# In the sliding-window attention stage, the gate's weight tile is taken ahead of the next head pair's scores on every engine

## The chip, the cores and the metric

The program runs on one core of one Trainium2 chip. The metric is the device time of one execution in microseconds (us). The engines named below are PE (TensorE, matrix products), DVE (VectorE), ACT (ScalarE), POOL (GpSimd) and SP (which issues the weight DMAs). Each engine works through its own list of instructions in order, and they meet only at semaphores. A difference under about 0.5% of the time (10.9 us) is not told apart from no change in this kernel.

## The reference

The program computes two blocks one after the other on 512 tokens of width 1024: first a block with a state-space branch, a recurrent branch and a memory attention, then a block of four layers (`second_block`). The change is in the second of those layers, a sliding-window attention with a gate. Cut to what matters:

```python
def sliding_window_attention(q, k, v, sinks, rel_bias):
    ...                                   # blocks of 128 queries see 256 keys
    s = jnp.einsum('bnqhgd,bnkhd->bnhgqk', qb, kb).astype(jnp.float32) * (HEAD_DIM ** -0.5)
    ...
    s = jnp.where(valid[None, :, None, None], s + bias, NEG_INF)
    sink = jnp.broadcast_to(sinks.astype(jnp.float32).reshape(SWA_KV_HEADS, grp, 1, 1), s.shape[:-1] + (1,))
    p = jax.nn.softmax(jnp.concatenate([s, sink], axis=-1), axis=-1)[..., :-1]
    o = jnp.einsum('bnhgqk,bnkhd->bnqhgd', p.astype(v.dtype), vb)
    return o.reshape(bsz, L, SWA_WIDTH)

def swa_branch(h, w_in, sinks, w_out, rel_bias):
    ...
    q, k, v, z = jnp.split(h @ w_in, [SWA_WIDTH, SWA_WIDTH + kv_w, SWA_WIDTH + 2 * kv_w], axis=-1)
    ...
    o = sliding_window_attention(q, k, v, sinks, rel_bias)
    return (o * jax.nn.silu(z)) @ w_out
```

There are 16 query heads of width 64, and 2 heads of keys and values. The gate is `silu(z)`, with `z` another 1024 columns of the same projection.

## The kernel before

All float32 weights come as "slabs" of 16 blocks of 128x128. SP loads a slab into a ring of three (L435). ACT copies it into a rounded high part (`ring_high`, L440) and DVE or POOL forms the remainder (`ring_low`, L445). A product of a weight tile with the activations is three matmuls for each of eight blocks (L483 to L485). A weight tile uses eight blocks, so a slab holds two tiles, and the split of a slab is issued behind every second tile (`split_high` on ACT, `split_low` on POOL in this stage). `split_high` waits until the tile that used the old high part has been computed.

`stage_swa` handles the heads as eight pairs j = 0 to 7 and is written out engine by engine, in a fixed order. Its parts for a pair are:

- scores(j), PE, L3061: query times key, into four PSUM banks `sb[j]`.
- logits(j), DVE, L3111 to L3122: scale and bias from PSUM into the tile `swa_s`, then maxima over keys (L3117, L3118) and three small operations. The last one, L3122, raises `mx`.
- exps(j), ACT, L3188 and L3193: exponentials with their sums. It waits for `mx` and raises `ex`.
- probs(j), DVE, L3127, L3128, L3131: divides by the sum. It waits for `ex` and raises `pn`.
- transposes(j), PE, L3079, wait for `pn`. ACT copies them to `swa_pt` (L3210, four copies), and PE multiplies them with the values (L3093) into the bank `ob[j]`. I call this last product PV(j).
- the gate's weight tile z(j), PE, L483 to L485, into bank `zb[j]`. DVE takes it out (evac_z, L1492), ACT makes the tanh (curve, L2899) and DVE the factor (L2904). The tanh has a single slot, so curve(j) waits for factor(j - 1).
- gated(j), DVE, L3144: output times factor, from `ob[j]`. Then ACT and DVE split the result (L2908, L2912) for the output projection, `gated_output`.

The scores of a pair are made two pairs ahead. In step j of the loop, PE does transposes(j), scores(j + 2), z(j + 2), PV(j). DVE does probs(j + 1), gated(j - 1), logits(j + 2), evac_z(j + 2), factor(j + 1), and the low part of j - 2. ACT does the four copies of pair j, exps(j + 2), the split of a slab when z(j + 2) ended one, curve(j + 2), and the high part of j - 1.

PSUM has eight banks, handed out in turn (`take_bank`), and a bank is reused only after its reader is done. In the steady steps the fourth score bank of pair j + 2 is the one that `ob[j - 1]` had, so the last quarter of the scores waits for gated(j - 1).

Of the kernel before, what the change touches and what calls it, by code (L numbers as in the profile page):

```python
# [28 lines left out]
KD = DM // P  # L29
# [3002 lines left out]
def stage_swa(C, L):  # L3032
# [3 lines left out]
    sb, pb, ob, zb = [[C.take_bank() for _ in range(TC)] for _ in range(2)], [], [], [C.take_tile(KD) for _ in range(2)]  # L3036
    for j in range(NJ):
        pb.append([C.take_bank() for _ in range(TC)])
        if j + 2 < NJ:
            sb.append([C.take_bank() for _ in range(TC)])  # L3040
            zb.append(C.take_tile(KD))
        ob.append(C.take_bank())
    mx, ex, pn = C.reserve("mx", NJ), C.reserve("ex", NJ), C.reserve("pn", NJ)
    zr = C.reserve("swaz", 1)
# [1 line left out]
    with C.stage() as block:  # L3046
        @block.sync
        def _(sp):
            C.load_slabs(sp, block.slabs)

        @block.tensor
        def _(pe):
            def scores(j):

                for b, u in enumerate(sb[j]):
                    e = b // 2
                    C.open(pe, u)
                    for n in (2 * (b % 2), 2 * (b % 2) + 1):
                        lo = 0 if n else P
                        r = slice(64 * e, 64 * e + 64)  # L3060
                        mm = pe.matmul(C.bank[u.b][:, n % 2 * 256 + lo:n % 2 * 256 + 256], L.Q[r, j, n * P:(n + 1) * P],  # L3061
                                       L.K[r, 0, (n - 1) * P + lo:(n + 1) * P], start=True, stop=True)
                    mm.then_inc(C.bank_full[u.b], 1)

            seen = set()
            C.read(pe, L.v_uses[-1])
            C.read(pe, L.k_tile)
            scores(0)
            scores(1)
            for j in range(2):  # L3070
                C.gemm(pe, zb[j], C.H.tiles(KD), seen)
            for j in range(NJ):
                pe.wait_ge(pn.sem, pn.at(j))
                for n, u in enumerate(pb[j]):
                    C.open(pe, u)
                    for e in range(2):
                        for kt in range(0 if n else 1, 2):
                            a = (2 * e + kt) * P
                            mm = pe.transpose(C.bank[u.b][:, a:a + P], L.S[:, j % 2, n, e, kt * P:(kt + 1) * P], C.ident[:])  # L3079
                    mm.then_inc(C.bank_full[u.b], 1)  # L3080

                if j + 2 < NJ:
                    scores(j + 2)
                    C.gemm(pe, zb[j + 2], C.H.tiles(KD), seen)
                u = ob[j]
                C.open(pe, u)
                for n in range(TC):
                    C.read(pe, pb[j][n])
                    for e in range(2):
                        first = 0 if n else 1  # L3090
                        for kt in range(first, 2):
                            a = (2 * e + kt) * P
                            mm = pe.matmul(C.bank[u.b][64 * e:64 * e + 64, n * P:(n + 1) * P],  # L3093
                                           L.V[:, n - 1 + kt, 64 * e:64 * e + 64], L.PT[:, n, a:a + P],
                                           start=(kt == first), stop=(kt == 1))
                mm.then_inc(C.bank_full[u.b], 1)

        @block.vector
        def _(dve):
# [35 lines left out]
            def evac_z(j):  # L3135
                u = zb[j][0]
                C.full(dve, u)
                times_root(dve, j, C.bank[u.b]).then_inc(C.bank_read[u.b], 1)
# [21 lines left out]
            for j in range(NJ):  # L3160
                if j + 1 < NJ:
                    probs(j + 1)
                if j > 0:
                    gated(j - 1)
                if j + 2 < NJ:
                    logits(j + 2)
                    evac_z(j + 2)
                if j + 1 < NJ:
                    gate.factor_on_dve(dve, j + 1, L.Z[:, j + 1, :], 1.0)
                if j > 1:  # L3170
                    gate.low_on_dve(dve, j - 2)
# [12 lines left out]
        def _(act):  # L3184
# [11 lines left out]
            def curve(j):  # L3196
                C.read(act, zb[j][0])
                gate.curve_on_act(act, j, L.Z[:, j, :], ACT.Tanh, 0.5)
# [6 lines left out]
            for j in range(NJ):  # L3205
                for n, u in enumerate(pb[j]):
                    C.full(act, u)
                    lo = 0 if n else 1
                    v = lambda ap: ap.rearrange("p (e t k) -> p e t k", e=2, t=2)[:, :, lo:2, :]
                    act.activation(v(L.PT[:, n, :]), v(C.bank[u.b][:]), ACT.Copy).then_inc(C.bank_read[u.b], 1)  # L3210
                if j + 2 < NJ:
                    exps(j + 2)
                    C.split_high(act, zb[j + 2][0])
                    curve(j + 2)
                if j > 0:
                    gate.high_on_act(act, j - 1)
            gate.high_on_act(act, NJ - 1)
# [650 lines left out]
```

## Time and profile before

| what | us |
|---|---|
| median of 3 runs | 2182.3 (2181.11 to 2189.23) |
| profiled execution, its own time | 2188.14 |
| its span | 2186.0 |
| PE / DVE / ACT / POOL busy in the span | 1996.6 / 1341.6 / 850.3 / 466.5 |

The profiled execution takes 2.14 us more than its span. The mean granted TensorE clock was 0.963 of full speed. The stage of the change lies between 1421 and 1536 us of the span, about 5% of it. A row of the timeline gives start, length, engine, line, operation, output and inputs, a count where equal instructions were merged, and in brackets how long the engine had been idle before and what ended the idle time. In rows of PE a matmul of the scores or of PV counts twice.

### The profile page before, as it was taken

How to read it: one execution, taken by the hardware profiler on the slowest of the kernel's cores; microseconds unless marked ns; L12 is line 12 of the kernel's file. 1: busy time of each engine (PE TensorE's matmuls, PEld its weight loads, DVE VectorE, ACT ScalarE, POOL GpSimd, SP SyncE). 2: the span in 40 equal slices, each digit the busy share in tenths (PEclk: the TensorE clock that was granted, in tenths of full speed). 3: DMA queues.
4: the chain of work that ended last, by engine and by line, in shares of the span. 5: the costliest groups of instructions: out<-in, count | busy, mean ns of one | idle time of the engine just before them, and what ended most of it. 6: DMA issues, size and time to landing. Idle time of an engine off the chain costs nothing.

```text
span 2186.0 us, 24847 instructions
## 1 busy us (share of the span) xinstructions
PE 1996.6 (91%) x9910; PEld 1567.2 (72%) x9910; DVE 1341.6 (61%) x1926; ACT 850.3 (39%) x1228; POOL 466.5 (21%) x393
## 2 busy tenths in 40 slices
PE   4998888999999999999999899988989989899986
PEld 3777665788657888768797676866777756578865
DVE  5997885825639245445566454678386476738474
ACT  3324646412259224422232343355342344435332
POOL 5861110323248603024400101012001011100001
PEclk9999998999999999999999999999998999999998
DMA  3333331233322434434546626211221210123211
GB/s 129 125 145 121 129 112 61 80 118 122 124 96 97 154 111 159 173 87 135 183 132 148 156 78 123 78 58 40 71 107 58 97 39 20 39 77 125 97 58 58
DMA packets 63746, 225.20 MB, mean 103 GB/s; under 512 B 14144, under 2 KB 31216, under 8 KB 43280
## 3 DMA queue, kind: packets, MB, share of 16 engines
q1 hardware_dynamic: 22896, 162.54, 21.2%
q0 software_dynamic: 19760, 45.83, 7.1%
q10 hardware_dynamic: 20976, 15.26, 3.3%
q8 instruction: 78, 1.28, 0.2%
q14 instruction: 36, 0.29, 0.0%
HBM read 208.72 MB, written 14.81 MB: 102 GB/s over the span
## 4 chain that ended last, share of the span: by engine, by line
PE 64%; DVE 10%; ACT 5%; issue 3%; ACTq 1%; DMA 1%; POOL 0%; DVEq 0%; POOLq 0%
PE bank L483 18%; PE bank L484 18%; PE bank L485 18%; PE bank L482 2%; DVE ring_low L445 1%; PE bank L3295 1%; PE bank L3322 1%; ACT ring_high L440 1%; ACTq L2476 1%; ACT swa_s L3193 1%; PE bank L2000 1%; DVE lru_x L1914 1%; PE bank L619 1%; DVE swa_s L3111 1%; PE bank L3309 1%
## 5 line engine op out<-in xcount | busy, mean ns | idle before, releaser
L483 PE MATMUL bank<-h_high,ring_high 128*128 128x512 f32 x1248 | 508.3, 407 | 36.3 <-DVE ring_low L445 12.2
L445 DVE TENSOR_TENSOR ring_low<-ring,ring_high 128x2048 fp32r<-128x2048 f32 x136 | 329.5, 2423 | 325.3 <-ACT ring_high L440 325.1
L484 PE MATMUL bank<-h_low,ring_high 128*128 128x512 f32 x1248 | 495.2, 397 | 0.0
L485 PE MATMUL bank<-h_high,ring_low 128*128 128x512 f32 x1248 | 494.8, 396 | 0.0
L440 ACT ACTIVATE ring_high<-ring 128x2048 fp32r<-128x2048 f32 x145 | 277.3, 1913 | 514.4 <-PE bank L485 511.8
L483 PEld LDWEIGHTS bank<-h_high,ring_high 128*128 128x128 f32 x1248 | 240.8, 193 | 106.4 <-issue 40.3
L484 PEld LDWEIGHTS bank<-h_low,ring_high 128*128 128x128 f32 x1248 | 240.7, 193 | 53.1 <-issue 4.1
L485 PEld LDWEIGHTS bank<-h_high,ring_low 128*128 128x128 f32 x1248 | 239.8, 192 | 51.9
L445 POOL TENSOR_TENSOR ring_low<-ring,ring_high 128x2048 fp32r<-128x2048 f32 x9 | 44.3, 4925 | 385.2 <-ACT ring_high L440 385.2
L483 PE MATMUL bank<-gated_high,ring_high 128*128 128x512 f32 x256 | 104.3, 407 | 8.3 <-DVE sq L3584 5.0
L484 PE MATMUL bank<-gated_low,ring_high 128*128 128x512 f32 x256 | 102.0, 398 | 0.0
L485 PE MATMUL bank<-gated_high,ring_low 128*128 128x512 f32 x256 | 101.6, 397 | 0.0
L483 PEld LDWEIGHTS bank<-gated_high,ring_high 128*128 128x128 f32 x256 | 49.0, 192 | 22.3 <-issue 7.5
L483 PE MATMUL bank<-ring_high,h_high 128*128 128x512 f32 (+1 forms) x160 | 60.4, 378 | 3.5 <-ACT u_tok L2610 2.1
L3433 ACT ACTIVATE mla_s<-mla_s,mla_st 128x128 f32<-128x128 f32 (+1 forms) x64 | 36.0, 563 | 64.3 <-DVE mla_st L3345 62.1
L1213 ACT ACTIVATE sq<-bank 128x512 f32<-128x512 f32 x32 | 19.3, 602 | 104.4 <-PE bank L485 104.4
L484 PE MATMUL bank<-ring_low,h_high 128*128 128x512 f32 (+1 forms) x160 | 59.8, 374 | 0.0
L485 PE MATMUL bank<-ring_high,h_low 128*128 128x512 f32 (+1 forms) x160 | 59.7, 373 | 0.0
L484 PEld LDWEIGHTS bank<-gated_low,ring_high 128*128 128x128 f32 x256 | 49.0, 191 | 11.7 <-issue 1.0
L485 PEld LDWEIGHTS bank<-gated_high,ring_low 128*128 128x128 f32 x256 | 48.8, 191 | 11.4
L669 DVE SCALAR_TENSOR_TENSOR sq<-bank,cols,sq 128x511 f32<-128x511 f32 (+2 forms) x72 | 53.9, 749 | 2.5
L3295 PE MATMUL bank<-mla_k,mla_q 128*128 128x128 f32 (+3 forms) x128 | 40.9, 467 | 14.3 <-ACT mla_k L3424 14.3
(517 smaller groups left out, 3859.8 us busy)
## 6 DMA issues: line engine op xcount, KB each, us to landing
ring<-slabs SPq DMA_DIRECT2D x149, 1024.0 KB, 4.8
acs_rows<-acs_rows POOLq DMA_DIRECT2D x16, 512.0 KB, 4.9
s_outputs<-s_ca POOLq DMA_DIRECT2D x4, 1152.0 KB, 5.0
x<-xT SPq DMA_DIRECT2D x2, 2048.0 KB, 8.5
exp_acs<-acs_rows POOLq DMA_DIRECT2D x16, 256.0 KB, 8.8
s_b<-s_br POOLq DMA_DIRECT2D x8, 512.0 KB, 4.2
s_rows<-s_powers POOLq DMA_DIRECT2D x16, 256.0 KB, 6.7
s_inputs<-s_w POOLq DMA_DIRECT2D x8, 512.0 KB, 3.0
```

What stands on the lines that cost most here:

```text
L440: act.activation(self.ring_high[:, self.splits_before[s] % AHEAD, :], self.ring[:, s % RING, :], ACT.Copy)\
L445: dve.tensor_tensor(self.ring_low[:, s % RING, :], self.ring[:, s % RING, :], self.ring_high[:, self.splits_before[s] % AHEAD, :].bitcast( ...
L482: return pe.matmul(out, w, x, start=start, stop=stop)
L483: pe.matmul(out, w[0], x[0], start=start, stop=False)
L484: pe.matmul(out, w[0], x[1], start=False, stop=False)
L485: return pe.matmul(out, w[1], x[0], start=False, stop=stop)
L619: pe.matmul(C.bank[u.b][:, 0:n], C.ones[:], C.sq[:, i % 4, 0:n], start=(k == 0), stop=(k == len(grp) - 1)).then_inc(summed.sem, 1)
L669: ins = dve.scalar_tensor_tensor(out=acc[:, d:T], in0=x[:, 0:T - d], scalar=w(3 - d), in1=acc[:, d:T], op0=ALU.mult, op1=ALU.add)
L1914: dve.tensor_tensor_scan(L.XL[:, m, :], L.R[:, m, :], q, 0.0, ALU.mult, ALU.add)\
L2000: mm = pe.matmul(C.bank[u.b][:], L.V[:, mt, a:a + P], L.PT[:, mt, :], start=(mt == 0), stop=(mt == 1))
L3295: mm = pe.matmul(C.bank[u.b][:, 0:(i + 1) * P], L.Q[:, h, i * P:(i + 1) * P], L.K[:, h % 4, 0:(i + 1) * P], start=True, stop=True)
L3433: ins = act.activation(s, s, ACT.Exp, bias=st[:, 0, i:i + 1], accum_out=st[:, 1, i:i + 1])
```

## The change

Four places swap two neighbours each. The instructions are the same, 7246 rows on PE, 1522 on DVE and 779 on ACT before and after. POOL's and SP's lists do not change. Banks are handed out in the new order too.

```diff
         pb.append([C.take_bank() for _ in range(TC)])
         if j + 2 < NJ:
+            zb.append(C.take_tile(KD))
             sb.append([C.take_bank() for _ in range(TC)])
-            zb.append(C.take_tile(KD))
         ob.append(C.take_bank())
...
                 if j + 2 < NJ:
+                    C.gemm(pe, zb[j + 2], C.H.tiles(KD), seen)
                     scores(j + 2)
-                    C.gemm(pe, zb[j + 2], C.H.tiles(KD), seen)
                 u = ob[j]
...
                 if j + 2 < NJ:
+                    evac_z(j + 2)
                     logits(j + 2)
-                    evac_z(j + 2)
                 if j + 1 < NJ:
                     gate.factor_on_dve(dve, j + 1, L.Z[:, j + 1, :], 1.0)
...
                 if j + 2 < NJ:
-                    exps(j + 2)
                     C.split_high(act, zb[j + 2][0])
                     curve(j + 2)
+                    exps(j + 2)
                 if j > 0:
                     gate.high_on_act(act, j - 1)
```

On ACT, this is the order in a step whose z tile ends a slab (j = 1, 3 or 5), rows that go with -, rows that come with +. L440 is the split, L2899 the curve, L3188 and L3193 the exponentials, L3210 the copies.

```order
 L3210 ACTIVATE swa_pt_162<-bank 128x512 x3
+L440 ACTIVATE ring_high_54<-ring_52 128x2048
+L2899 ACTIVATE root_57<-swa_z_163 128x512
 L3188 ACTIVATE swa_st_164<-swa_st_164 128x8
 L3193 ACTIVATE swa_s_161,swa_st_164<-swa_s_161,swa_st_164 128x128 x2
 L3193 ACTIVATE swa_s_161,swa_st_164<-swa_s_161,swa_st_164 128x256 x6
-L440 ACTIVATE ring_high_54<-ring_52 128x2048
-L2899 ACTIVATE root_57<-swa_z_163 128x512
 L2908 ACTIVATE gated_high_169<-swa_y_160 128x512
```

The split and the curve have moved from behind the exponentials to the place ahead of them. In steps 0, 2 and 4 the curve moves alone.

On DVE, the order in step 1, from gated(0) on. L1492 is evac_z, L3111 opens the logits, L3122 closes them, L2904 is the factor of the pair before, L3127 opens the next probs.

```order
 L3131 TENSOR_TENSOR swa_s_161<-swa_s_161,swa_st_164 128x2048
 L3144 SCALAR_TENSOR_TENSOR swa_y_160<-bank,swa_z_163 128x512
+L1492 TENSOR_TENSOR swa_z_163<-bank,norm_root_72 128x512
 L3111 SCALAR_TENSOR_TENSOR swa_s_161<-bank,st_63,swa_bias_159 128x128
 L3111 SCALAR_TENSOR_TENSOR swa_s_161<-bank,st_63,swa_bias_159 128x256 x3
...
 L3121 TENSOR_TENSOR swa_st_164<-cols_58,swa_st_164 128x8
 L3122 TENSOR_SCALAR swa_st_164<-swa_st_164 128x8
-L1492 TENSOR_TENSOR swa_z_163<-bank,norm_root_72 128x512
 L2904 SCALAR_TENSOR_TENSOR swa_z_163<-root_57,swa_z_163 128x512
 L3127 TENSOR_TENSOR swa_st_164<-swa_st_164 128x8
```

The evacuation has moved ahead of the logits. The factor has stayed behind them.

## Rows read from the trace of the kernel before

**Rows 1.** The page, part 4: shares of the chain that ended last
```profile
PE 64%; DVE 10%; ACT 5%; issue 3%; ACTq 1%; DMA 1%; POOL 0%; DVEq 0%; POOLq 0%
```

**Rows 2.** Windows: busy PE, PEld, DVE, ACT, POOL; clock; DMA
```profile
1461.10:1467.10 6.00, 5.95 (x13) 4.30 (x14) 5.51 (x13) 0.00 (x0) 0.00 (x0) 0.50 0.00 0
...
1495.60:1509.00 13.40, 11.85 (x83) 9.49 (x82) 10.79 (x20) 8.42 (x25) 5.33 (x1) 1.00 0.23 79
```

**Rows 3.** Waits, 1425 to 1545 us (waiter, awaited, us, times, longest)
```profile
DVE swa_st L3127 <- ACT swa_s L3193: 8.1, 5, 2.8
...
PE bank L3061 <- DVE swa_y L3144: 8.5, 4, 3.9
```

**Rows 4.** Timeline, DVE, one steady step
```profile
1499.02 0.17 DVE L3127 TENSOR_TENSOR swa_st<-swa_st 128x8 f32<-128x8 f32 x1 [1.35 <-ACT swa_s L3193]
...
1501.67 0.68 DVE L3144 SCALAR_TENSOR_TENSOR swa_y<-bank,swa_z 128x512 f32<-128x512 f32 x1
1502.58 2.96 DVE L3111 SCALAR_TENSOR_TENSOR swa_s<-bank,st,swa_bias 128x128 f32<-128x128 f32 x8 [0.23 <-DVE swa_y L3144]
...
1507.91 0.17 DVE L3120 TENSOR_TENSOR swa_st<-swa_st,cols 128x8 f32<-128x8 f32 x1
...
1509.24 0.69 DVE L1492 TENSOR_TENSOR swa_z<-bank,norm_root 128x512 f32<-128x512 f32 x1 [0.76 <-PE bank L485]
1509.85 0.68 DVE L2904 SCALAR_TENSOR_TENSOR swa_z<-root,swa_z 128x512 f32<-128x512 f32 x1
...
1512.48 0.17 DVE L3127 TENSOR_TENSOR swa_st<-swa_st 128x8 f32<-128x8 f32 x1 [1.35 <-ACT swa_s L3193]
```

**Rows 5.** Timeline, ACT: the same step, and a curve that waited
```profile
1445.40 0.63 ACT L2899 ACTIVATE root<-swa_z 128x512 f32<-128x512 f32 x1 [1.12 <-DVE swa_z L2904]
...
1508.52 0.21 ACT L3188 ACTIVATE swa_st<-swa_st 128x8 f32<-128x8 f32 x1 [4.98 <-DVE swa_st L3122]
...
1512.36 0.61 ACT L2899 ACTIVATE root<-swa_z 128x512 f32<-128x512 f32 x1
1512.88 0.61 ACT L2908 ACTIVATE gated_high<-swa_y 128x512 fp32r<-128x512 f32 x1
```

**Rows 6.** Timeline, PE, the same step
```profile
1502.40 1.13 PE L3061 MATMUL bank<-swa_k,swa_q 64*128 64x256 f32 x4 [1.55 <-DVE swa_y L3144]
1503.46 0.50 PE L483 MATMUL bank<-h_high,ring_high 128*128 128x512 f32 x1
...
1508.82 0.39 PE L485 MATMUL bank<-h_high,ring_low 128*128 128x512 f32 x1
1509.13 1.80 PE L3093 MATMUL bank<-swa_pt,swa_v 128*64 128x128 f32 x28
1510.86 1.75 PE L3079 MATMUL bank<-ident,swa_s 128*128 128x128 f32 x14
```

**Rows 7.** Timeline, PE and DVE, the first two steps
```profile
1440.41 3.22 PE L3079 MATMUL bank<-ident,swa_s 128*128 128x128 f32 x14 [2.42 <-DVE swa_s L3131]
...
1457.76 0.17 DVE L3127 TENSOR_TENSOR swa_st<-swa_st 128x8 f32<-128x8 f32 x1 [2.80 <-ACT swa_s L3193]
...
1461.15 2.07 PE L3061 MATMUL bank<-swa_k,swa_q 64*128 64x256 f32 x4 [3.94 <-DVE swa_y L3144]
```

**Rows 8.** Timeline, DVE, ACT, POOL and PE, the end of the stage
```profile
1525.94 0.17 DVE L3127 TENSOR_TENSOR swa_st<-swa_st 128x8 f32<-128x8 f32 x1 [1.35 <-ACT swa_s L3193]
...
1527.79 5.27 POOL L445 TENSOR_TENSOR ring_low<-ring,ring_high 128x2048 fp32r<-128x2048 f32 x1 [21.59 <-ACT ring_high L440]
...
1528.66 1.80 ACT L3210 ACTIVATE swa_pt<-bank 128x256 f32<-128x256 f32 x4
...
1529.16 3.23 PE L3093 MATMUL bank<-swa_pt,swa_v 128*64 128x128 f32 x28 [3.10 <-ACT swa_pt L3210]
1529.42 4.18 DVE L2904 SCALAR_TENSOR_TENSOR swa_z<-root,swa_z 128x512 f32<-128x512 f32 x1
...
1535.73 0.50 PE L483 MATMUL bank<-gated_high,ring_high 128*128 128x512 f32 x1
```

## The prediction, written before the changed kernel was run

> **What bounds the kernel now.** I began with the page. Its chain of what ended last belongs to PE for 64% of the span [rows 1], so most stages are bound by matmuls. A share over the whole span says nothing of this stage, so I took it alone, first by windows. In one steady step of 13.4 us PE is busy 11.85, DVE 10.79 and ACT 8.42 us [rows 2]: no engine is full, so a loop that passes from engine to engine must set the step. The waits name its two seams [rows 3]. DVE's L3127 (probs) waited five times for ACT's exponentials, 8.1 us in all. PE's scores waited four times for DVE's L3144 (gated), 8.5 us in all.
>
> The timelines then show which of the two closes the loop. DVE begins a probs at 1499.02 and the next at 1512.48, one step of 13.46 us [rows 4]. Between them stand, with no slack:
> - probs(j + 1) from 1499.02 to 1501.67: 2.65.
> - gated(j - 1) to the first logits instruction at 1502.58: 0.91 [rows 4].
> - logits(j + 2), to 1508.52, when ACT starts on them: 5.94 [rows 4, 5].
> - exps(j + 2) on ACT, to 1512.48: 3.96 [rows 4, 5].
>
> The sum is 13.46. It is a loop of DVE and ACT alone, because probs(j + 2) of the next step must have exps(j + 2). While ACT makes the exponentials, DVE does evac_z, factor and the low part and still idles 0.76 and 1.35 us. So evac_z and factor cost nothing today: exps hide them. On ACT the curve is behind the exponentials, at 1512.36 [rows 5], and costs nothing either. PE's wait of 1.55 us [rows 6] is a consequence: it waits for a member of this loop.
>
> **The change, part by part, in a steady step.** Four things move, and the question for each is on which side of exps it comes to stand.
>
> 1. evac_z moves ahead of logits. It leaves the shadow of exps and enters the loop. From its start to the next instruction are 0.61 us (1509.24 to 1509.85) [rows 4]. Its wait (0.76 for the weight tile) goes if z is ready, which part 3 checks. Bounds: 0.61, or 0.69, its length. I take 0.61.
>
> 2. On ACT the curve moves ahead of exps, and it waits for factor(j + 1), since the tanh has one slot. That factor stands behind logits(j + 2) on DVE and has not moved. So exps(j + 2) can no longer start when the logits are done: DVE first makes the factor (0.68 long, 1509.85 [rows 4]; it starts about 0.1 before ACT would have started, as successive DVE rows overlap, so 0.58), hands over to ACT (0.10: the factor that ended at 1445.30 released the curve of 1445.40 [rows 5]), and ACT makes the curve (0.52, from 1512.36 to 1512.88 [rows 5]). Together 1.20. Below, this term can't be nothing, since the wait is a semaphore's; above, with full lengths (0.68 + 0.10 + 0.61), it is 1.39. I take 1.20, since starts are what follow each other.
>
>    The new step is 13.46 + 0.61 + 1.20 = 15.27 us, with probs at D and: evac_z at D + 3.56, logits from D + 4.17 to D + 10.1, exps from D + 11.3 to D + 15.27.
>
> 3. z(j + 2) moves ahead of scores(j + 2) on PE. PV(j) stands behind the scores, and it is now the third score bank, not the fourth, that `ob[j - 1]` had. PE therefore waits with two score banks of four still to do until gated(j - 1) ends, D + 3.4, then does those two banks (1.06), PV(j) (1.73), transposes(j + 1) (1.7) and z(j + 3) (5.7) [rows 6], and is through with z at D + 13.6. DVE wants it at 15.27 + 3.56 = D + 18.8. The slack is 5.2 us, so z is never late at full clock and the 0.76 us go. The remaining two score banks follow at once, and PE idles for some 3.8 us a step.
>
>    After 3.94 us of idling the granted clock was 0.50 for 6.0 us [rows 2, 7], which is 1.2 GHz. Six such us do 3 us less work, and the slack covers it. At 1.55 us it had stayed full [rows 6]. So I expect low stretches in most steps, at no cost in the loop.
>
> 4. The split moves ahead of curve and exps in steps 1, 3 and 5. It waits for the end of z(j + 2), reached at D - 1.7, or D + 1.3 after a low stretch, and ACT comes to it at about D + 2.3, behind the high part and the four copies. Behind it on ACT stand curve and exps, which wait for DVE until D + 10.7 anyway, so it costs nothing. POOL's subtraction starts with the end of the split, near D + 4.2. SP's load of the next slab hangs on the end of a z tile, which comes no later in the step. POOL's and SP's own lists do not change.
>
> **A rule on the port.** At the end of the stage before, DVE's L2904 took 4.18 us instead of 0.68. It ended with POOL's subtraction (1527.79 + 5.27 = 1533.06), 0.54 after it [rows 4, 8]. The logits' L3111, which reads one operand from PSUM, ran in 2.96 us beside another such subtraction, without a stall [rows 2, 4]. The Trainium skill (SBUF — State Buffer, section "Who interferes with whom") says that a DVE instruction with two SBUF inputs and a GpSimd instruction that reads SBUF hold one port pair in turn, and the later one is blocked to the end. The trace agrees. By that rule POOL's subtraction must not reach the two-input rows behind the logits' reductions, L3120 on. From rows: the subtraction takes 5.27 and would end at D + 9.5, while L3120 comes at D + 4.17 + 5.33 (1502.58 to 1507.91) = D + 9.5 [rows 4, 8]. It just passes; if it did not, the price would be what it overshoots, three times. By the row alone or by the rule my sum stays.
>
> **The first step and the end.** In step 0 there is no gated. PE's transposes end at 1443.6 [rows 7]. z(2) follows at once and takes 5.75 (1503.46 to 1508.82 + 0.39 [rows 6]), to 1449.4. Then evac_z 0.61, logits 5.94, factor, hand-over and curve 1.20, exps 3.96: probs of step 1 start at 1461.1 instead of 1457.76 [rows 7], 3.3 later. Five steps of 15.27 lead to step 6 at 1537.45. Before, it was 1525.94 [rows 8]. Shift: +11.5.
>
> At the end something comes back. Before, ACT had the last split, a curve and a high part between the exponentials and the copies of pair 6: copies at 1528.66, 2.72 behind the probs of 1525.94 [rows 8]. Now only a high part (0.52) stands there, so the copies and PV(6) are 2.2 earlier. Against that, PE has idled for over 8 us by then. PV(6) took 3.23 instead of 1.80 after 3.10 of idling [rows 6, 8], and this time the low clock may also hold for transposes(7), up to 1.5 more. I take 0.7, half way. L2904's stall of 3.5 us goes, and was hidden: the output projection at 1535.73 followed PE's own work without a gap.
>
> Sum: 11.5 - 2.2 + 0.7 = +10.0 us. Behind the stage the output projection is bound by PE and starts that much later, and nothing there absorbs it. The profiled execution would go from a span of 2186.0 (2188.14 with what lies around it) to 2196.0 (2198.1). The profiled run was 5.8 above the median, within the spread of the runs, so I add the difference to the median: 2182.3 + 10.0 = 2192.3 us.
>
> **Rivals.**
> - *z comes late (slower).* If the low clock outlasts the slack, it decides: it must hold for more than 10.4 us, double the slack of 5.2, where 6.0 is the longest that I measured [rows 2]. With PE at 1.2 GHz through its whole step (2.07 + 3.23 + 3.22 + twice 5.75 [rows 7, 8]) z ends at D + 23.4, 4.6 late, and POOL's subtraction then falls on L3120. A step without idling follows and recovers, so it strikes at most three steps: +14, to 2206. For it: PE idles each step. Against it: the length of the measured stretch.
> - *The added links are hidden (no change).* If the loop kept its 13.46, because DVE's 2.1 us of idling absorbed what moves, step 1 would start 2.1 later, step 6 at 1527.2 (+1.3), and the end gives 2.2 back: -0.9, 2181.4 us. For it: DVE does idle that long. Against it: the idle time lies behind logits, while evac_z is added ahead of them, and the curve's wait is real.
> - *PE's waits were the bound (faster).* PE's own work in a step is 11.85 [rows 2] against 13.46. With z ahead of the wait for `ob`, six steps could save 1.6 each, and 2.2 at the end: -11.8, 2170.5. For it: the 8.5 us of PE's waits [rows 3]. Against it: the loop above closes without PE.
>
> **Chances.** Forecast mechanism 0.80, z late 0.10, hidden 0.06, PE's bound 0.04. The forecast's own range is 2189 to 2196 (the bounds of factor and curve, 0.19 a step over six steps, the clock at the end -0.7 to +0.8, and the noise of a median). The limit of what can be told from no change, 0.5%, lies at +10.9 us, just above my value, so its 0.80 splits into 0.45 within and 0.35 slower. Faster is 0.04, within 0.45 + 0.06 = 0.51, slower 0.35 + 0.10 = 0.45. The range goes from 2185 to 2201: it reaches towards the hidden case and part of the way to the late one.
>
> **What would show it.** Right: probs (L3127) every 15.2 to 15.3 us, ACT's curve (L2899) waiting for DVE's factor and L3188 following it without a wait, evac_z with no wait for PE, PE idle 3 to 4 us ahead of the last score banks with the clock at half after it, copies of pair 6 half a us behind exps. Wrong: a step near 13.5; L1492 waiting for PE; L3120 or L2904 of several us beside POOL's L445; ACT's L440 waiting for a slab; or the output projection later than the stage's last matmuls explain.

## The result, and the profile after

The kernel before took 2184.41 us in six runs beside the changed kernel (2181.11 to 2190.55), the changed kernel 2196.61 us (2193.76 to 2203.53). The ratio is 1.0057, with an interval of 1.0035 to 1.0079: slower by about 12 us (7.6 to 17.3). The forecast was 2192.3 us, +10.0, from the three runs of before that were known then (2182.3); of the 4.3 us between 2192.3 and 2196.61, 2.1 are the higher median of six runs. The intervals here reach 0.11 to 0.25% to each side, so smaller differences than the 0.5% named at the start can be told.

| | before | after |
|---|---|---|
| span of the profiled execution, us | 2186.0 | 2193.5 |
| mean granted clock | 0.963 | 0.963 |
| transposes(0) to the output projection, us | 95.32 | 107.40 |
| the same, worked out ahead | | 105.3 |

The stage is 12.08 us longer (1437.70 to 1545.10, against 1440.41 to 1535.73 [rows 7, 8]). The span grew by only 7.5, since in this one execution the stage began 2.7 us earlier and what stands behind it was 1.9 shorter. Neither place holds an instruction that the change touches. So below I compare lengths within the stage, and call the first one **the stage length**.

The timeline of DVE after, one steady step, answers to [rows 4]:

```profile
1505.30 0.17 DVE L3127 TENSOR_TENSOR swa_st<-swa_st 128x8 f32<-128x8 f32 x1 [3.98 <-ACT swa_s L3193]
...
1507.95 0.68 DVE L3144 SCALAR_TENSOR_TENSOR swa_y<-bank,swa_z 128x512 f32<-128x512 f32 x1
1508.85 0.69 DVE L1492 TENSOR_TENSOR swa_z<-bank,norm_root 128x512 f32<-128x512 f32 x1 [0.21 <-DVE swa_y L3144]
1509.46 2.95 DVE L3111 SCALAR_TENSOR_TENSOR swa_s<-bank,st,swa_bias 128x128 f32<-128x128 f32 x8
...
1515.19 0.17 DVE L3122 TENSOR_SCALAR swa_st<-swa_st 128x8 f32<-128x8 f32 x1
1515.27 0.68 DVE L2904 SCALAR_TENSOR_TENSOR swa_z<-root,swa_z 128x512 f32<-128x512 f32 x1
...
1520.54 0.17 DVE L3127 TENSOR_TENSOR swa_st<-swa_st 128x8 f32<-128x8 f32 x1 [3.98 <-ACT swa_s L3193]
```

Probs starts at 1505.30 and at 1520.54, a step of 15.24 where 15.27 was worked out. DVE now idles 3.98 us ahead of probs, where it idled 0.76 and 1.35 us behind the logits before. The timeline of ACT after, which answers to [rows 5]:

```profile
1500.81 0.63 ACT L2899 ACTIVATE root<-swa_z 128x512 f32<-128x512 f32 x1 [7.29 <-DVE swa_z L2904]
1501.35 0.19 ACT L3188 ACTIVATE swa_st<-swa_st 128x8 f32<-128x8 f32 x1
...
1505.18 0.62 ACT L2908 ACTIVATE gated_high<-swa_y 128x512 fp32r<-128x512 f32 x1
1505.70 1.80 ACT L3210 ACTIVATE swa_pt<-bank 128x256 f32<-128x256 f32 x4
```

The curve waits for DVE's factor, and the exponentials follow without a wait of their own. This is part 2 of the prediction. The waits of the stage after, 1425 to 1550 us, answer to [rows 3]:

```profile
ACT root L2899 <- DVE swa_z L2904: 49.6, 7, 9.0
DVE swa_st L3127 <- ACT swa_s L3193: 25.1, 6, 4.6
...
PE bank L3061 <- DVE swa_y L3144: 9.3, 5, 2.9
...
DVE swa_s L3111 <- PE bank L3061: 1.6, 4, 0.5
```

The wait to see is the last and smallest. Most of ACT's 49.6 us is idle time that it had before too, with another name: L3188 waited 45.6 us for DVE's L3122 then. The 1.6 us of DVE are new, and no step of the prediction has them. One of the four, 0.23 us, is in step 0, and the others are in the odd steps. Probs of steps 1 to 6 started at 1458.53, 1474.30, 1489.53, 1505.30, 1520.54 and 1536.30: steps of 15.77, 15.23, 15.77, 15.24 and 15.76. The timelines of PE and of DVE after, in a long step and then in a short one:

```profile
1492.92 3.35 PE L3061 MATMUL bank<-swa_k,swa_q 64*128 64x128 f32 x8 [2.86 <-DVE swa_y L3144]
...
1508.69 1.78 PE L3061 MATMUL bank<-swa_k,swa_q 64*128 64x128 f32 x8 [0.65 <-DVE swa_y L3144]
```

```profile
1493.68 2.17 DVE L3111 SCALAR_TENSOR_TENSOR swa_s<-bank,st,swa_bias 128x128 f32<-128x128 f32 x6
1496.30 0.88 DVE L3111 SCALAR_TENSOR_TENSOR swa_s<-bank,st,swa_bias 128x256 f32<-128x256 f32 x2 [0.45 <-PE bank L3061]
```

And the windows after, with busy PE, PEld, DVE, ACT and POOL and then the clock: the long step, the short step, and the last two score banks in each.

```profile
1489.53:1505.30 15.77, 12.91 (x74) 10.51 (x73) 10.79 (x20) 8.48 (x25) 4.52 (x1) 0.78 0.17 64
1505.30:1520.54 15.24, 14.59 (x94) 11.67 (x93) 10.70 (x21) 6.70 (x24) 0.00 (x0) 1.00 0.03 4
1492.90:1496.30 3.40, 3.38 (x10) 2.36 (x12) 2.78 (x7) 0.63 (x1) 2.70 (x1) 0.50 0.00 0
1508.69:1510.40 1.71, 1.71 (x8) 1.26 (x8) 1.55 (x4) 0.00 (x0) 0.00 (x0) 1.00 0.00 0
```

In the long step PE has idled 2.86 us, and the clock stands at 0.50 (1.2 GHz) behind it. The two banks then take 3.35 us and DVE, which reads them as logits, catches up and waits 0.45. In the short step PE idled 0.65, the clock is 1.00 (2.4 GHz), and the banks take 1.78. A mean of 0.78 over the long step is about 6.9 us at the half clock. The two banks and PV(j) run slowly in them (3.35 and 2.98 us, against 1.78 and 1.80) and make PE's z tile later, so that PE idles little in the next step and keeps the full clock, is early again and idles 2.9 us in the one behind: it alternates.

The end of the stage after (DVE, ACT, PE) answers to [rows 8]:

```profile
1536.30 0.17 DVE L3127 TENSOR_TENSOR swa_st<-swa_st 128x8 f32<-128x8 f32 x1 [3.97 <-ACT swa_s L3193]
...
1539.78 0.69 DVE L2904 SCALAR_TENSOR_TENSOR swa_z<-root,swa_z 128x512 f32<-128x512 f32 x1
```

```profile
1536.69 1.80 ACT L3210 ACTIVATE swa_pt<-bank 128x256 f32<-128x256 f32 x4
```

```profile
1537.20 3.28 PE L3093 MATMUL bank<-swa_pt,swa_v 128*64 128x128 f32 x28 [5.47 <-ACT swa_pt L3210]
1540.41 3.03 PE L3079 MATMUL bank<-ident,swa_s 128*128 128x128 f32 x14
1543.37 1.80 PE L3093 MATMUL bank<-swa_pt,swa_v 128*64 128x128 f32 x28
1545.10 0.50 PE L483 MATMUL bank<-gated_high,ring_high 128*128 128x512 f32 x1
```

The copies start 0.39 behind the last probs (2.72 before), L2904 no longer stalls, and the projection follows 8.80 behind that probs (9.79 before). PV(6) and transposes(7) run at a granted clock of 0.50 and 0.54.

So the 12.08 us are: +0.02 up to probs of step 0, +3.46 in step 0 (15.99 against 12.53), +9.59 in steps 1 to 5 (77.77 against 68.18), and -0.99 at the end.

### The profile page after: what moved, and what is told of

It reads as the page before. It is cut to its first block, busy times and chain, and to the rows that moved or that the text cites. A ratio compares the mean times of both kernels' runs of the same rounds, so it can differ in the third digit from the quotient of the medians.

```text
span 2193.5 us, 24847 instructions
## 1 busy us (share of the span) xinstructions
PE 1998.8 (91%) x9910; PEld 1571.6 (72%) x9910; DVE 1339.2 (61%) x1926; ACT 850.4 (39%) x1228; POOL 463.6 (21%) x393
## 4 chain that ended last, share of the span: by engine, by line
PE 63%; DVE 11%; ACT 5%; issue 3%; ACTq 1%; DMA 1%; POOL 0%; DVEq 0%; POOLq 0%
PE bank L483 18%; PE bank L484 17%; PE bank L485 17%; PE bank L482 2%; DVE ring_low L445 2%; PE bank L3295 1%; PE bank L3322 1%; ACT ring_high L440 1%; ACTq L2476 1%; ACT swa_s L3193 1%; PE bank L2000 1%; DVE lru_x L1914 1%; PE bank L619 1%; DVE swa_s L3111 1%; DVE swa_st L3118 1%
## 5 line engine op out<-in xcount | busy, mean ns | idle before, releaser
L445 DVE TENSOR_TENSOR ring_low<-ring,ring_high 128x2048 fp32r<-128x2048 f32 x136 | 329.5, 2424 | 324.8 <-ACT ring_high L440 324.6
L440 ACT ACTIVATE ring_high<-ring 128x2048 fp32r<-128x2048 f32 x145 | 277.4, 1913 | 514.0 <-PE bank L485 507.9
L445 POOL TENSOR_TENSOR ring_low<-ring,ring_high 128x2048 fp32r<-128x2048 f32 x9 | 41.2, 4578 | 386.4 <-ACT ring_high L440 386.4
L1213 ACT ACTIVATE sq<-bank 128x512 f32<-128x512 f32 x32 | 19.3, 603 | 104.2 <-PE bank L485 104.2
L482 PE MATMUL bank<-lru_x,ring 128*128 128x512 f32 x112 | 50.0, 609 | 3.6 <-DVE lru_x L1789 3.6
```

The lines of the kernel that those rows point to most:

```text
L440: act.activation(self.ring_high[:, self.splits_before[s] % AHEAD, :], self.ring[:, s % RING, :], ACT.Copy)\
L445: dve.tensor_tensor(self.ring_low[:, s % RING, :], self.ring[:, s % RING, :], self.ring_high[:, self.splits_before[s] % AHEAD, :].bitcast( ...
L482: return pe.matmul(out, w, x, start=start, stop=stop)
```

## The experiments

The theory: a loop of DVE and ACT sets the step, what stands between its members costs its full length, and what stands behind DVE's logits is free as long as exps cover it. On top of it, PE costs time in the changed kernel only where its low clock falls on the two banks behind `ob`.

### Undoing single parts of the change

**e1_act_back**, the changed kernel with ScalarE's order of before:

```diff
                 if j + 2 < NJ:
+                    exps(j + 2)
                     C.split_high(act, zb[j + 2][0])
                     curve(j + 2)
-                    exps(j + 2)
```

> The changed kernel, with ACT alone put back: exponentials first, then the split and the curve. My theory (the step is a loop of DVE and ACT, and the change lengthened it by evac_z ahead of the logits, 0.61 us, and by factor, hand-over and curve ahead of the exponentials, 1.20 us): the 1.20 go, steps of 13.46 + 0.61 = 14.07 us from probs to probs, at most 14.6 where PE is at the low clock; against the kernel before +4.5 to +6 us, so about 6 us under the changed kernel. Rival (PE's idling and its low clock make the loss, by late score banks): steps stay near 15.2 to 15.8, and the time that of the changed kernel, +12.

Measured: 2188.88 us, ratio 1.0023 (1.0012 to 1.0035), which is +4.2 us against the kernel before in the runs beside it, stage length 100.96 (+5.6). Steps of 14.24, 14.07, 14.06, 14.06 and 14.04. That is 13.46 + 0.61, the price of evac_z in the loop. The rest of a changed step is the order on ACT: 15.24 - 14.06 = 1.18 (1.20 worked out).

**e2_factor_first**, the changed kernel with the factor ahead of the evacuation on VectorE:

```diff
                 if j > 0:
                     gated(j - 1)
+                if j + 1 < NJ:
+                    gate.factor_on_dve(dve, j + 1, L.Z[:, j + 1, :], 1.0)
                 if j + 2 < NJ:
                     evac_z(j + 2)
                     logits(j + 2)
-                if j + 1 < NJ:
-                    gate.factor_on_dve(dve, j + 1, L.Z[:, j + 1, :], 1.0)
```

> The changed kernel, with DVE's factor(j + 1) ahead of evac_z and logits, so that the curve on ACT has nothing behind the logits to wait for. My theory: the curve is hidden beside the logits, the exponentials start right behind them, and the factor stands in the loop for 0.60: steps of 13.46 + 0.61 + 0.60 = 14.67 us (15.2 where PE is at the low clock), +6.5 to +8 us against before. Rival (the order of ACT's own work costs, curve and split ahead of the exponentials, whatever they wait for): steps stay at 15.2 to 15.8.

Measured: 2188.64 us, ratio 1.0025 (1.0010 to 1.0039). Four steps of 14.59 to 14.60, 0.08 under the 14.67 worked out, and one of 14.94. The stage length is 100.37 (+5.05), below what was expected, because the transposes of pair 0 ran at the full clock here (1.75 us) and at half in the kernel before (3.22 [rows 7]). This comes of itself from run to run, and is taken up at the end. Handover and curve are out of the loop in this order. The factor adds 0.53 to the 14.06 of e1: it takes 0.61 from its start to the next row's (1487.72 to 1488.33), and it starts 0.83 behind gated, where evac_z started 0.90 behind it in the changed kernel.

**e3_pe_busy** asks whether the 0.53 us of the long steps are the low clock. It gives PE more work in its idle time:

```diff
-                    for n in (2 * (b % 2), 2 * (b % 2) + 1):
+                    for n in (2 * (b % 2), 2 * (b % 2) + 1) * (4 if b == 1 and j > 2 else 1):
```

> The changed kernel, with more work on PE: the two matmuls of the second score bank are made four times over instead of once for pairs 3 to 7, some 2.5 us a step, in the stretch in which PE idles. Theory of the clock (steps of 15.77 alternate with 15.23 because the two last score banks run at 1.2 GHz after the idling and the last comes 0.45 late for the logits): PE no longer idles 2 to 3 us, the clock stays full, every step is 15.23, and the stage ends 1.6 us earlier than in the changed kernel. Rival (the 0.45 us are a wait of order, for a bank, and not of the clock): steps still alternate, or get longer by what PE has more to do.

Measured: 2194.47 us, ratio 1.0036 (1.0019 to 1.0052), stage length 103.73, which is 3.7 less than in the changed kernel, with more work in it. The intervals of e3 and of the changed kernel overlap, so it is the trace that tells them apart, and not the whole time. All steps are 15.21 to 15.23. The windows of two steps, with PE's waits and DVE's logits from the timelines of e3:

```profile
1496.00:1526.40 30.40, 29.88 (x189) 24.49 (x188) 21.34 (x41) 15.11 (x48) 4.54 (x1) 1.00 0.10 36
```

```profile
1506.87 4.37 PE L3061 MATMUL bank<-swa_k,swa_q 64*128 64x128 f32 x20
1511.50 1.78 PE L3061 MATMUL bank<-swa_k,swa_q 64*128 64x128 f32 x8 [0.26 <-DVE swa_y L3144]
```

```profile
1512.27 2.95 DVE L3111 SCALAR_TENSOR_TENSOR swa_s<-bank,st,swa_bias 128x128 f32<-128x128 f32 x8
```

PE hardly idles, the clock stays at 1.00, the two banks take 1.78 and L3111 doesn't wait. The missing term is the low clock on these two banks. A slab's split and POOL's subtraction also fall in the odd steps alone, which would be another reason for the alternation. But e3 has them in the same steps (POOL's rows at 1466.00, 1496.96 and 1527.41), and these steps are as short as the others. Of the 3.7 us, 1.66 are the steps 1 to 5, 1.45 step 0, where the transposes were at the full clock, and the rest the end.

### Doing single parts alone

**e4_act_only**, the kernel before with the changed order on ScalarE and nothing else:

```diff
                 if j + 2 < NJ:
-                    exps(j + 2)
                     C.split_high(act, zb[j + 2][0])
                     curve(j + 2)
+                    exps(j + 2)
```

> The kernel before, with ACT's part of the change alone: split and curve ahead of the exponentials, PE and DVE as before. My theory: the curve now waits for evac_z and factor, which stand behind the logits and behind the weight tile that PE makes late in the step (10.2 us after the probs at full clock, 13.1 after an idle stretch), and ACT's exponentials stand behind that. Steps of 16.1 to 16.6 us if the clock holds, and about 19 if PE's longer idling brings it down each step; +17 to +33 us in all. Rival (only the place of evac_z and PE's order cost, ACT's order is free): steps stay near 13.5 and the time that of before.

Measured: 2209.84 us, ratio 1.0116 (1.0092 to 1.0141), steps of 18.61 to 19.69, stage length 123.72 (+28.4). A timeline of ACT in e4, then one of PE:

```profile
1507.04 1.91 ACT L440 ACTIVATE ring_high<-ring 128x2048 fp32r<-128x2048 f32 x1 [10.34 <-PE bank L485]
1508.85 0.61 ACT L2899 ACTIVATE root<-swa_z 128x512 f32<-128x512 f32 x1
1509.37 0.19 ACT L3188 ACTIVATE swa_st<-swa_st 128x8 f32<-128x8 f32 x1
```

```profile
1497.88 2.07 PE L3061 MATMUL bank<-swa_k,swa_q 64*128 64x256 f32 x4 [4.17 <-DVE swa_y L3144]
```

Here the exponentials stand behind a split that waits for the whole z tile, and the tile stands behind a score bank that waits for gated. A loop through all three engines closes, at 19 us. In the changed kernel, with PE's and DVE's order changed as well, z is ready and this loop is gone. So ACT's part of the change costs less where the others are there.

**e5_pe_only**, the kernel before with the order and the banks of the changed PE:

```diff
         if j + 2 < NJ:
+            zb.append(C.take_tile(KD))
             sb.append([C.take_bank() for _ in range(TC)])
-            zb.append(C.take_tile(KD))
...
                 if j + 2 < NJ:
+                    C.gemm(pe, zb[j + 2], C.H.tiles(KD), seen)
                     scores(j + 2)
-                    C.gemm(pe, zb[j + 2], C.H.tiles(KD), seen)
```

> The kernel before, with the change's part on PE and in the order of banks alone (z ahead of the scores); DVE and ACT as before. My theory: the loop of DVE and ACT is untouched, so steps stay near 13.46, but evac_z stays behind the logits and frees a bank that the next transposes need, so PE gets a loop of its own (evac, transposes 0.8, z 5.7, first scores 0.8, logits 5.94, evac 0.6): steps of about 13.9 us; with 2.1 us lost in the first step, +4 to +5 us in the stage. Rival (the order on PE makes the loss of the change): steps of 15.2 to 15.8 as in the changed kernel.

Measured: 2196.27 us, ratio 1.0034 (1.0018 to 1.0050), steps of 15.86, 14.22, 15.81, 14.23 and 14.23, stage length 104.61 (+9.3). The expectation had the right loop and the wrong size, 13.9 and +4 to +5: a miss. The timelines of PE and of DVE in e5:

```profile
1488.58 1.09 PE L3079 MATMUL bank<-ident,swa_s 128*128 128x128 f32 x8 [2.65 <-DVE swa_z L1492]
```

```profile
1497.69 3.09 DVE L3111 SCALAR_TENSOR_TENSOR swa_s<-bank,st,swa_bias 128x128 f32<-128x128 f32 x8 [2.43 <-PE bank L3061]
```

The transposes need z's bank, and it comes free with evac_z, which still stands behind the logits. PE waits 2.65 us for it in every step, z(j + 3) and the scores are late, and DVE waits 0.85 or 2.43 for them. At the full clock the loop closes at 14.23, where 13.9 had been worked out. Behind the wait of 1488.58 the clock was low (0.81 over the 9.1 us that follow), z was 1.6 later and the step 15.81; behind that of 1474.35 it had stayed at 1.00. The expectation had no low clock in it. e1 differs from e5 by evac_z's place alone and has steps of 14.06. So evac_z ahead of logits pays 0.61 in the loop and takes this wait away.

### Shortening the loop of the kernel before

If the loop is what counts, gated (0.91) can be taken out of it. It stands there only because a score bank is `ob`'s.

**e6_gated_behind**, the kernel before with `ob` in two banks of its own and gated behind the factor:

```diff
+    own = ((C.next_bank + 6) % 8, (C.next_bank + 7) % 8)
+    C.pinned = own
...
-        ob.append(C.take_bank())
+        ob.append(C.take_given(own[j % 2]))
+    C.pinned = ()
...
-                if j > 0:
-                    gated(j - 1)
                 if j + 2 < NJ:
                     logits(j + 2)
                     evac_z(j + 2)
                 if j + 1 < NJ:
                     gate.factor_on_dve(dve, j + 1, L.Z[:, j + 1, :], 1.0)
+                if j > 0:
+                    gated(j - 1)
```

> The kernel before, with the outputs of PV in two banks of their own (the other six go round among the rest), and gated(j - 1) on DVE moved from ahead of the logits to behind factor, into the shadow of the exponentials. The rule that I draw from the loop (what stands between logits and exponentials' end is free, what stands elsewhere on DVE costs its full time) says: the 0.91 us of gated leave the loop, steps of 12.55 us; where a slab's split on ACT holds up the copies that PE now waits for, z gets about 1 us late and steps are up to 13.6. In the stage -3.5 to -6 us. Rival (PE with 11.85 us of work a step is already the bound and the seam to PE costs as much as it saves): steps of 13.4 to 14, no gain.

Measured: 2186.06 us, ratio 0.9998 (0.9986 to 1.0010), stage length 97.00 (+1.7). Three steps are 12.54 to 13.17, but two are 14.86 and 14.85. A miss. The timelines of ACT, PE and DVE of e6 in a long step (its lines are 3 further down than in the kernel before: L3213 the copies, L3064 the scores):

```profile
1493.16 1.89 ACT L440 ACTIVATE ring_high<-ring 128x2048 fp32r<-128x2048 f32 x1
...
1496.00 1.80 ACT L3213 ACTIVATE swa_pt<-bank 128x256 f32<-128x256 f32 x4
```

```profile
1496.42 1.78 PE L3064 MATMUL bank<-swa_k,swa_q 64*128 64x128 f32 x8 [1.68 <-ACT swa_pt L3213]
1498.13 0.50 PE L483 MATMUL bank<-h_high,ring_high 128*128 128x512 f32 x1
1499.19 0.63 PE L483 MATMUL bank<-h_high,ring_high 128*128 128x512 f32 x1
```

```profile
1505.50 0.69 DVE L1492 TENSOR_TENSOR swa_z<-bank,norm_root 128x512 f32<-128x512 f32 x1 [3.44 <-PE bank L485]
```

The split stands ahead of the copies that PE waits for. PE idles 1.68 us, the clock is 0.81 from 1496.42 to 1505.50, and evac_z waits 3.44 for z.

**e7_gated_and_act** is e6 with the split behind the copies:

```diff
                     act.activation(v(L.PT[:, n, :]), v(C.bank[u.b][:]), ACT.Copy).then_inc(C.bank_read[u.b], 1)
+                if j == NJ - 2:
+                    curve(j + 1)
+                if 0 < j < NJ - 1:
+                    C.split_high(act, zb[j + 1][0])
+                if 0 < j < NJ - 2:
+                    curve(j + 1)
+                if j > 1:
+                    gate.high_on_act(act, j - 2)
                 if j + 2 < NJ:
                     exps(j + 2)
-                    C.split_high(act, zb[j + 2][0])
-                    curve(j + 2)
-                if j > 0:
-                    gate.high_on_act(act, j - 1)
-            gate.high_on_act(act, NJ - 1)
+            for j in (NJ - 2, NJ - 1):
+                gate.high_on_act(act, j)
```

> As e6, and on ACT the split of a slab, the curve and the high part stand behind the copies of the next pair and ahead of its exponentials, one step later than in the kernel before, where nothing waits for them: copies start right behind the exponentials. My theory: steps of 12.55 to 12.8 us all along, the copies of pair 6 some 2.7 us earlier, and the end of the stage 2.7 to 3.6 us shorter; in the stage -7 to -9 us, some 2176 us. Rival (the port): POOL's subtraction now starts about 3.6 us behind probs and reaches L3120 of DVE, which takes two inputs from SBUF: L3120 waits for its end, 0.2 to 1 us in steps 2 and 4. Rival (order of ACT is free anyway): as e6.

Measured: 2178.01 us, ratio 0.9959 (0.9944 to 0.9973), faster than both kernels. Steps of 13.18, 12.61, 12.55, 12.59 and 12.55, and 13.46 - 0.91 = 12.55. The stage length is 88.22 (-7.1). The window of one step of e7, and DVE in it (L3130 is probs, L3114 the logits, L3147 gated):

```profile
1490.67:1503.22 12.55, 12.55 (x83) 10.02 (x83) 10.70 (x21) 8.48 (x24) 3.29 (x1) 1.00 0.23 85
```

```profile
1492.89 0.68 DVE L2904 SCALAR_TENSOR_TENSOR swa_z<-root,swa_z 128x512 f32<-128x512 f32 x1
1493.49 0.68 DVE L3147 SCALAR_TENSOR_TENSOR swa_y<-bank,swa_z 128x512 f32<-128x512 f32 x1
...
1496.38 0.17 DVE L3130 TENSOR_TENSOR swa_st<-swa_st 128x8 f32<-128x8 f32 x1 [1.36 <-ACT swa_s L3196]
...
1499.02 2.95 DVE L3114 SCALAR_TENSOR_TENSOR swa_s<-bank,st,swa_bias 128x128 f32<-128x128 f32 x8
```

PE is busy for the whole 12.55 us, at the full clock: a shorter loop would probably find PE as its bound, which no run here tests. The rival of the port did come, but small: in steps 2 and 4 the row that is L3120 in the kernel before took 0.23 and 0.22 us instead of 0.17 beside POOL's row, and these steps are the 12.61 and 12.59. Behind the stage, e7 gives back 1.0 us in the projection, as e9 does below.

**e10_act_late** is the other half of e7, ScalarE's order alone (the diff of e7 without that of e6).

> The kernel before with nothing but e7's order on ScalarE: copies(j), the split of z(j+1), curve(j+1), the high part of j-2, the next exponentials. VectorE's order and the banks stay, so gated stands in the loop behind probs. Theory (the loop of VectorE and ScalarE sets the step, and e7 gained 0.9 a step by taking gated out of it): the steps stay at 13.4 to 13.5, only the end is shorter by 2.4 to 3.6 us as in e8; the stage is 92 to 93 us long and the time 2182 to 2184.5, a ratio of 0.998 to 0.9995. Rival (e7's gain came from ScalarE's order, and the banks and gated's place did nothing): steps of 12.5 to 12.7, stage about 88, time about 2178.

Measured: 2186.34 us, ratio 1.0003 (0.9992 to 1.0014), steps of 13.88, 13.83, 13.64, 13.46 and 13.63, stage length 93.31 (-2.0, with the transposes of pair 0 at the full clock). So e7's gain does not come from this order alone, nor from the banks and gated's place alone (e6): it needs both. The time did not show the small gain that I had forecast, 1.0 of which goes again in the projection (next). The steps are up to 0.4 longer than expected, for two reasons. In three of them evac_z waits 3.20, 2.37 and 2.35 us for z, at a mean clock of 0.87 in the middle one. That is not this order's doing: e9 (next) has the order of before in these steps, and has the same ones, 13.88, 13.66 and 13.64, with waits of 3.21, 2.38 and 2.36. The step of 13.83 is the port. A row of DVE in it, and POOL's:

```profile
1475.17 0.54 DVE L3120 TENSOR_TENSOR swa_st<-swa_st,cols 128x8 f32<-128x8 f32 x1
```

```profile
1471.06 4.62 POOL L445 TENSOR_TENSOR ring_low<-ring,ring_high 128x2048 fp32r<-128x2048 f32 x1 [31.65 <-ACT ring_high L440]
```

L3120 takes 0.54 instead of 0.17 and ends 0.03 behind POOL's row. The 0.37 us are what the step is longer than 13.46. It is the collision that the prediction had priced and that the changed kernel missed by 1.4 us or more.

### The end of the stage

**e8_end_curve_first**, the kernel before with curve(7) right behind the copies of pair 6:

```diff
+                if j == NJ - 2:
+                    curve(j + 1)
+                    C.split_high(act, zb[j + 1][0])
                 if j + 2 < NJ:
                     exps(j + 2)
+                if j + 3 < NJ:
                     C.split_high(act, zb[j + 2][0])
                     curve(j + 2)
```

> The kernel before with only the end of the stage changed on ACT: behind exps(7) come the copies of pair 6, and then curve(7) and the last split. My theory: PE's PV(6) starts 1.0 us behind the last probs instead of 3.2, at full clock if the idling of about 1 us is too short to bring it down; the output projection starts 6.2 to 7.6 us behind the last probs instead of 9.8; POOL's subtraction starts after factor(7), which takes its 0.68 us. Steps as before, 13.46. Rival: the end is bound by DVE's chain (probs, gated, factor, low parts), and the output projection starts or stalls at the same distance.

**e9_end_split_first** swaps the first two lines that e8 adds: the split, then the curve.

> The kernel before with the end of ScalarE's queue as in e8, but with the last split ahead of curve(7): copies(6), split(7), curve(7). So GpSimd's subtraction starts before VectorE's last factor. Theory (the two engines shut each other out of the State Buffer): GpSimd starts about 4.1 us behind the last probs and takes some 4.5; factor(7), which reads two tiles of the State Buffer, comes at about 4.7 to 5.0 and is held until GpSimd is done, so its row is 3.5 to 4.5 us long as in the kernel before (4.18), where it took 0.69 in e8. The output projection still begins about 7.4 to 7.6 behind the last probs, but the gated half and the low half of the last tile are late, its first parts of the weight stall it, and the time lies 1 to 3 us above that of e8. Rival (the 4.18 is the operation's own, or a wait on something else): factor(7) takes 0.69 beside GpSimd and nothing stalls. The loop's steps stay at 13.46 by both.

Measured, in one run each: e8 2183.2 us, the projection 7.41 behind the last probs, stage length 92.93 (-2.4). e9 2188.8 us, the projection 7.51 behind it, stage length 92.95. The timelines of DVE and POOL at the end of e8, and of e9:

```profile
1527.66 0.69 DVE L2904 SCALAR_TENSOR_TENSOR swa_z<-root,swa_z 128x512 f32<-128x512 f32 x1
...
1528.87 0.68 DVE L3144 SCALAR_TENSOR_TENSOR swa_y<-bank,swa_z 128x512 f32<-128x512 f32 x1
1529.70 4.23 DVE L2912 TENSOR_TENSOR gated_low<-swa_y,gated_high 128x512 fp32r<-128x512 f32 x1
```

```profile
1528.78 4.60 POOL L445 TENSOR_TENSOR ring_low<-ring,ring_high 128x2048 fp32r<-128x2048 f32 x1 [24.35 <-ACT ring_high L440]
```

```profile
1532.44 4.64 DVE L2904 SCALAR_TENSOR_TENSOR swa_z<-root,swa_z 128x512 f32<-128x512 f32 x1 [1.32 <-ACT root L2899]
```

```profile
1531.97 4.56 POOL L445 TENSOR_TENSOR ring_low<-ring,ring_high 128x2048 fp32r<-128x2048 f32 x1 [24.09 <-ACT ring_high L440]
```

L2904 takes 0.69 us ahead of POOL and 4.64 beside it, and in these two runs the instruction with two tiles of SBUF that comes to stand beside L445 takes the blow: in e8 it is L2912. Both end 0.55 us behind POOL's row. L3144, with one operand in PSUM, took 0.68 in e8 beside the same POOL row. From the first matmul of the projection to the first ACT row that reads its result (L1213) are 5.90 us in e8 and in the kernel before, and 7.01 in e9. So the stall costs 1.1 us there, near the lower end of what I expected. What I had not expected are e9's steps 1 to 5, of 13.88, 13.46, 13.66, 13.45 and 13.64, where e8 with the same orders has 14.30 and four of 13.46 or 13.47. In the two of 13.66 and 13.64 the clock fell behind 1.4 to 1.6 us of idling, at which it stayed full in e8 and in the kernel before, and z came late. Single runs can't tell the rest of the 5.6 us between e8 and e9: runs of the kernel before beside e9 lay between 2180.89 and 2189.6.

## Why the prediction was right, and what it missed

- **The loop of 13.46 us: right, at the full clock.** e1 (+0.60) and e7 (-0.91) moved the step by the length of what was put in or taken out, and e2's factor by 0.53. It is not the only bound of the kernel before: its step 1 took 14.33 us, because the clock fell behind PE's wait of 3.94 [rows 7], evac_z waited 3.66 us for z, and probs then followed with no wait for ACT. The prediction started from measured times of probs, so this does not touch its sum, but PE's waits were not worth nothing there.
- **Part 1, evac_z 0.61: right**, measured 0.60 in e1.
- **Part 2, factor, handover and curve 1.20: right**, 1.18 between e1 and the changed kernel's short steps. Step 0 was 15.99 where 15.87 had been worked out.
- **Part 3, z in time: right.** L1492 never waited for PE in steps 1 to 5, though the clock was low. In step 0 it waited 1.12 us, as the sum for that step has it.
- **Part 3, "two banks (1.06)" and low stretches "at no cost in the loop": wrong.** This is the mis-sized term. The 1.06 was read from a row of x4 [rows 6], which is one bank and not two; two take 1.78. I then set the low clock against the slack of z, 5.2 us, and not against that of the banks that come first behind the idle time. DVE wants the last of them at D + 6.3 (1495.85 in the step of 1489.53). At the full clock they are done at D + 5.2, at the half clock at D + 6.7. The wait is 0.45, the step 0.53 longer, in three steps 1.6 us. e3 showed that this goes with the clock.
- **The clock "in most steps": half right.** It fell in the odd steps and recovered in the even ones. PE idled 2.86 and 0.65 us in turn, and not some 3.8 in each.
- **Part 4, the split free, and POOL clear of L3120: right.** POOL's rows were 4.52 us, not 5.27, and ended 1.4 to 2.0 us ahead of L3120. e10 shows what the collision costs where it comes.
- **The end, -2.2 + 0.7: too good.** Measured -0.99. The copies came 2.33 earlier, but PV(6) and transposes(7) both ran slowly (3.28 and 3.03): the low clock took 1.3, not 0.7. PE had idled 5.47 us by then, not over 8.
- **The rivals.** None came. The half of "z comes late" that did is its reason: idle time that costs speed behind it. It struck where I had not looked.

Of the 2.1 us that the forecast lacked in the stage, 1.4 are in steps 1 to 5, 0.5 at the end, and 0.15 in step 0. That the 12.08 us of the stage and the 12.2 us between the medians agree so well is partly luck, since the interval of the latter is 7.6 to 17.3.

On the rule of the port: before, L2904 took 4.18 beside POOL [rows 8]; e8 and e9 turn this on and off by the order alone. The Trainium skill (SBUF — State Buffer, section "Who interferes with whom") says that a DVE instruction with two SBUF inputs and a GpSimd instruction that reads SBUF exclude each other, and that the one issued second is blocked until the first is done. The runs agree, for these lines, and with e10's L3120.

## What to carry to other kernels

Look for the loop across engines before pricing a move. An instruction within it costs its full length, one in the shadow of another engine's member costs nothing, and a wait that looks large may belong to an engine outside it. Price every instruction that is moved ahead of another by what its semaphore waits for (the curve was 0.52 long and cost 1.18), and every bank by who frees it. Where an engine idles longer than before, ask what its first instruction behind the idle time feeds, since that is where a low clock lands.

## What the runs showed of the chip that I had not expected

- More work made the steps shorter: with e3's extra matmuls the clock was at 1.00 from 1496.00 to 1526.40, and steps 1 to 5 lost 1.66 us.
- The same idle time does not always give the same clock. Behind 2.4 us of idling, transposes(0) took 3.22 us in the kernel before, and about as long in five other traces, but 1.75 in e2, e3, e4, e6, e9 and e10, with nothing changed ahead of it. This shifts a stage by 1.4 us from run to run, so single profiles were compared by steady steps here. It reaches the steady steps too: behind 1.42 us of idling the clock was 1.00 in the kernel before (1488.90 to 1495.70) and 0.80 in e9 (1490.43 to 1498.78). Why it falls in one run and not in the other stays open.
- POOL's L445 has no fixed length: 4.52 to 4.62 us in the changed kernel, e7 and e10, where it started clear of DVE instructions with two tiles of SBUF, and 6.17, 5.33 and 5.27 in the kernel before [rows 8], where it started 1.74, 0.88 and 0.88 us ahead of the end of L3131, which is one. Counted from that end the three are 4.4 us each, so here it is POOL that was held.
